# The recurrence's value projection of heads 2 and 3 moved from the stage ahead of the first mixer's slots into eight of the slots

## The chip, the core and the metric

The kernel runs on one core of a Trainium2 chip. A core has engines with an instruction stream of their own: TensorE (PE, matrix products into the accumulators called PSUM), VectorE (DVE), ScalarE (ACT), GpSimd (POOL) and the queue engine SyncE (SP), which issues transfers from the chip's memory into the core's on-chip memory. They run in parallel and wait for each other by semaphores. The metric is the device time of one execution in microseconds (us); lower is better.

## What is computed

The program is a small transformer of several layers in fp32 over 512 tokens (256 of context, 256 of latents). The change is in the first mixer, of which this is what matters: a windowed attention and a gated recurrence of four heads, both fed by slices of one projection, and joined by one output product.

```python
def even_mixer(h_ctx, h_lat, w_in, w_out, qk_g, sink, out_g, lb, cos, sin, need_ctx):
    ...
    p = split_parts(h_lat @ w_in, EVEN_PARTS)      # a_q a_k a_v b_q b_ff b_fb b_i b_g
    ...
    a_lat = window_attention(q_lat, k_lat, kv_heads(p['a_v']), k_ctx, v_ctx, sink)
    ...
    k_fw, lf_fw = gates(p['b_ff'])
    k_bw, lf_bw = gates(p['b_fb'])
    q_l = jax.nn.silu(to_heads(p['b_q'], HGRN_HEADS).astype(F32))
    i_l = to_heads(p['b_i'], HGRN_HEADS).astype(F32)
    o_fw, _ = gla_chunked(q_l, k_fw, i_l, lf_fw, s_fw)
    o_bw, _ = gla_chunked(flip(q_l), flip(k_bw), flip(i_l), flip(lf_bw), s_bw)
    b_lat = gated_head_norm(o_fw + flip(o_bw), p['b_g'], out_g)
    y_lat = jnp.concatenate([a_lat.astype(dt), b_lat.astype(dt)], axis=-1) @ w_out
```

`b_i` is the value of the recurrence: 512 columns, 128 for each of the four heads, for all 512 tokens. Head h's values are needed first where its chunk states are updated.

## The kernel before

Every engine's program is written out by hand; nothing is reordered, so each engine runs its instructions as they stand. A planner, `make_plan`, only counts: it gives each product (a "job") a PSUM bank in turn from a pool, notes which engine empties the bank (`A` for ScalarE, `V` for VectorE), and from which job on a weight tile may be overwritten. The next job in a bank waits until the job before it in that bank was emptied (`bank`). Weights come into a ring of two tiles (`RING`), loaded by SP in the order of use; `load` waits until the tile's last reader is done.

Ahead of the mixer's slots stands a stage of whole projections on TensorE: the attention's queries (`even_q`, 4 token tiles x 8 matmuls of 512 columns), its keys and values (8 products of 128 columns), the recurrence's values (`even_bi`, 4 x 8 x 512 columns), its output gates (`even_bg`, the same), and the transposes of queries and keys (`even_qkT`). `by_token` makes them, one job for each token tile. Beside it, VectorE multiplies and adds 1 MB pieces of modulation weights ("slabs", L2862): two slabs lie on chip, SP issues slab i when slab i-2 was used (`load_slabs`), on the same queue as the ring's weights. Halfway VectorE norms and rotates queries and keys (L3030 to L3066), then it goes on with slabs, and only behind the last but one of them comes its part of the slots. At two places of the stage TensorE sums a modulation group over partitions (L1332) and turns it (L1319), for which it needs VectorE's slabs and ScalarE's copies.

Then come 48 slots. The even slots 0 to 30 start an attention pair each (scores L1547, softmax on VectorE and ScalarE from L3213 and L2414, transposes L1559, output L1572); scores of the next pair wait until ScalarE has read the last pair's. Slots 0 to 31 carry in between the projections of the four recurrence heads (`fill_at`, L1589): three matmuls of 512 columns a slot, three jobs for each head (forget gates forward and backward, queries), with a ring tile of 3 x 128 columns for each head. The heads' recurrence runs a round behind the projections (`heads_at`): keys by token and scores (L1475, L1488), updates of the chunk states (L1498, the first reader of the head's values `hv`), outputs (L1508, L1515). The states are chained on VectorE (L3147, L3149). Slots 33, 34, 35, 36, 37, 40, 43 and 46 (`PARTS`) hold eight parts of the first half of the output product (`out_block`, L1538, 4 matmuls of 512 columns each), which VectorE adds to the residual (`residual_part`, L3194). In the slots the pool of banks is two: jobs take bank 0 and bank 1 in turn, whatever they are.

Of the kernel before, what the change touches and what calls it, by code (L numbers as in the profile page):

```python
# [14 lines left out]
P = 128  # L15
D = 1024
KD = D // P
# [86 lines left out]
class Plan:  # L104
# [18 lines left out]
    def add(self, stage, engine):  # L123

        b = self.pool[self.turn % len(self.pool)]
        self.turn += 1
        self.own[stage].append(self.jobs)
        self.who += engine
        self.bank.append(b)
        self.before.append(self.last.get(b))  # L130
        self.last[b] = self.jobs
        self.jobs += 1
# [123 lines left out]

def fill_at(slot):

    return [] if slot >= UNITS else [divmod(3 * (slot % PER_ROUND) + n, KD) for n in range(3)]
# [73 lines left out]
def make_plan():  # L333
# [24 lines left out]
    for slot in range(SLOTS):  # L358
# [3 lines left out]
        for j, k in fill_at(slot):  # L362
            if (j, k) == (0, 0):
                a.start(f"head{slot // PER_ROUND}")
            if k == 0:
                a.add(f"head{slot // PER_ROUND}", "A")
            if (j, k) == (2, KD - 1):
                a.tile_used()
        if slot == CAT_SLOT:
            a.start("even_out_a")  # L370
# [87 lines left out]
def first_then_second_block(nc, a, out):  # L458
# [3 lines left out]
    with ExitStack() as ctx:  # L462
# [81 lines left out]
        ePT = [view(A0 + 5120, 512), ring[:, pl.tile["even_out"] // 2 % RING, 3072:3584]]  # L544
# [256 lines left out]
        def _(sp):  # L801
# [22 lines left out]
            def load(*parts, halves=2):  # L824
# [8 lines left out]
                for p in reversed(parts):  # L833
# [4 lines left out]
                    sp.dma_start(dst, p).then_inc(signal, 96 // len(parts))  # L838
# [39 lines left out]
            for lo in (2304, 2816):  # L878
                load(wcols(ew, lo, lo + 512))
            for h in range(HG):  # L880
                load(*(wcols(ew, lo + P * h, lo + P * h + P) for lo in (1280, 1792, 768)))
# [121 lines left out]
        def _(pe):  # L1003
# [445 lines left out]
            for _ in range(2):  # L1449
                by_token(BOTH, 512, where="even")  # L1450
# [41 lines left out]
            def updates(h, d):  # L1492
                w = 2 * h + d
                pe.wait_ge(hg_kts, w + 1)
                pe.wait_ge(hg_ss, 3 * h + d + 1)
                for c in range(8):
# [78 lines left out]

            for slot in range(SLOTS):
# [6 lines left out]
                for j, kk in fill_at(slot):  # L1583
                    if (j, kk) == (0, 0):
                        stage(f"head{slot // PER_ROUND}")
                        hw = weights(3 * P)
# [3 lines left out]
                    if kk == KD - 1:  # L1590
                        ins.then_inc(acc_full, 1)
                if slot < UNITS:
# [535 lines left out]
        def _(act):  # L2128
# [203 lines left out]
            for i in BOTH:  # L2332
                evac(hv[:, i, :], 512)
# [68 lines left out]

            for slot in range(SLOTS):
                raw_inputs(slot)
                if slot == 3:
# [412 lines left out]
        def _(dve):  # L2818
# [371 lines left out]
            def residual_part(f):  # L3190

                y = filled("even_out_a", f + 1)
                for c in (1, 0):
# [798 lines left out]
```

## Time and profile before

| | us |
|---|---|
| time before, median of 3 runs | 2555.9 (2553.59 to 2556.48) |
| span of the profiled execution | 2552.4 |
| stage ahead of the slots, first product of `even_q` to the first of slot 0, on TensorE | 40.4 to 143.3 |
| slots, on TensorE | 143.3 to 352.6 |
| TensorE busy | 2481.8 (97% of the span) |
| VectorE busy | 1672.4 (66%) |
| ScalarE busy | 657.5 (26%) |

The profile lists no time of the profiled execution other than its span; the median lies 3.5 us above the span, for what is ahead of the first and behind the last recorded instruction. Only the first 390 us bear on the change. The share of 97% is an average: in the slots TensorE has idle stretches of 0.2 to 1.9 us, each with the engine that ended it. A timeline row gives the start, the length, the engine and line, the operation with its tiles and shapes, the number of instructions, and in brackets the idle time before it and what ended that. An fp32 matmul shows as two records. A row of windows gives, for a stretch, its length, the busy time of the engine asked for, the clock granted to TensorE as a share of the full one, the busy share of the transfer engines and the GB/s they moved.

### The profile page before, as it was taken

The numbers are of one execution on the slowest core, as the hardware profiler recorded it, in microseconds if no ns is written. First come the engines' busy times: TensorE is split into PE (matmuls) and PEld (weight loads), VectorE is DVE, ScalarE is ACT, GpSimd is POOL, SyncE is SP. The second block draws the span as 40 slices with busy tenths as digits, with TensorE's granted clock in tenths as the row PEclk, the third lists the DMA queues.
The fourth block names the chain that finished last, engine by engine and source line by source line (L and its number), as shares of the span: only waits on it lengthen the run. The fifth ranks groups of instructions, "written<-read, shape, count | busy, mean of one in ns | idle before, by whom it ended". The sixth has DMA issues, their size and how long they took to land.

```text
span 2552.4 us, 41132 instructions
## 1 busy us (share of the span) xinstructions
PE 2481.8 (97%) x16726; PEld 2005.8 (79%) x16726; DVE 1672.4 (66%) x3298; ACT 657.5 (26%) x1760; POOL 73.0 (3%) x96
## 2 busy tenths in 40 slices
PE   6999899999999999999999999999999999999999
PEld 3545458888888886599996867869997877868999
DVE  4967767655777645466673787657773777647785
ACT  3145512111101111122212153333321135333320
POOL 0000000000000001000000001100000000110000
PEclk9999999999999999999999999999999999999999
DMA  8532115555575868245544424135654344125563
GB/s 341 187 118 48 44 34 182 154 177 167 188 272 184 289 209 322 71 130 152 169 163 149 165 73 127 68 119 143 172 170 145 132 124 108 68 87 146 166 178 120
DMA packets 342651, 386.78 MB, mean 152 GB/s; under 512 B 8110, under 2 KB 285190, under 8 KB 330176
## 3 DMA queue, kind: packets, MB, share of 16 engines
q1 hardware_dynamic: 330896, 320.89, 40.1%
q0 software_dynamic: 8832, 57.26, 6.4%
q10 hardware_dynamic: 2736, 6.01, 0.6%
q8 instruction: 133, 2.18, 0.4%
q14 instruction: 54, 0.44, 0.1%
HBM read 383.08 MB, written 1.05 MB: 150 GB/s over the span
## 4 chain that ended last, share of the span: by engine, by line
PE 84%; DVE 9%; issue 3%; ACT 3%; DMA 2%; ACTq 0%; DVEq 0%; SPq 0%
PE acc L1032 33%; PE mx L1032 14%; PE acc L1083 10%; PE acc L1071 9%; PE acc L1093 5%; PE acc L1589 2%; PE acc L1538 1%; PE mx L1947 1%; DVE arena L3905 1%; PE mx L1398 1%; DVE hT L2894 1%; PE mx L1934 1%; PE mx L2006 1%; PE mx L1422 1%; DMA ring<-in_mod_w 0%
## 5 line engine op out<-in xcount | busy, mean ns | idle before, releaser
L1032 PE MATMUL acc<-arena 128*128 128x128 f32 (+1 forms) x2248 | 353.8, 300 | 1.0 <-ACT gate L2507 0.5
L1032 PEld LDWEIGHTS acc<-arena 128*128 128x128 f32 x2248 | 310.0, 192 | 16.8 <-ACT gate L2507 0.9
L2862 DVE SCALAR_TENSOR_TENSOR arena<-mod_w,vcols,arena 128x2048 f32<-128x2048 f32 x98 | 228.4, 2348 | 61.2 <-DMA mod_w<-in_w_ada 46.0
L1083 PE MATMUL acc<-hT,ring 128*128 128x256 f32 (+1 forms) x1024 | 249.8, 406 | 0.8 <-DVE arena L3579 0.8
L1083 PEld LDWEIGHTS acc<-hT,ring 128*128 128x128 f32 x1024 | 194.1, 190 | 54.1 <-issue 29.4
L1032 PE MATMUL acc<-hT,ring 128*128 128x128 f32 (+1 forms) x1368 | 206.1, 301 | 2.8 <-ACT hT L2255 1.4
L3255 DVE TENSOR_TENSOR arena<-ring 128x512 f32<-128x512 f32 (+1 forms) x136 | 91.7, 674 | 178.3 <-PE acc L1032 173.8
L1032 PEld LDWEIGHTS acc<-hT,ring 128*128 128x128 f32 x1368 | 184.8, 191 | 16.1 <-issue 6.4
L1071 PE MATMUL acc<-ring,hT 128*128 128x512 f32 x448 | 194.1, 593 | 2.2 <-ACT hT L2164 1.3
L1032 PE MATMUL acc<-arena,ring 128*128 128x128 f32 (+1 forms) x1256 | 194.2, 298 | 0.0
L1032 PEld LDWEIGHTS acc<-arena,ring 128*128 128x128 f32 x1256 | 171.1, 192 | 7.7 <-issue 0.8
L1032 PE MATMUL mx<-hT,ring 128*128 128x128 f32 (+1 forms) x1152 | 174.4, 296 | 1.0 <-ACT arena L2543 0.9
L1071 PEld LDWEIGHTS acc<-ring,hT 128*128 128x128 f32 x448 | 84.5, 190 | 108.7 <-issue 103.9
L1032 PEld LDWEIGHTS mx<-hT,ring 128*128 128x128 f32 x1152 | 154.9, 192 | 7.6 <-ACT arena L2543 1.2
L1032 PE MATMUL mx<-arena,ring 128*128 128x128 f32 (+1 forms) x960 | 152.7, 301 | 0.0
L1032 PE MATMUL acc<-hT,arena 128*128 128x128 f32 (+1 forms) x888 | 141.0, 302 | 0.0
L1032 PEld LDWEIGHTS mx<-arena,ring 128*128 128x128 f32 x960 | 132.8, 192 | 8.2 <-issue 2.5
L1032 PEld LDWEIGHTS acc<-hT,arena 128*128 128x128 f32 x888 | 123.6, 192 | 6.0
L1093 PE MATMUL acc<-ring,hT 128*128 128x256 f32 x384 | 96.4, 388 | 2.0 <-ACT hT L2288 0.7
L3259 DVE TENSOR_TENSOR arena<-ring 128x512 f32<-128x512 f32 (+1 forms) x136 | 92.0, 677 | 4.7
L3261 DVE TENSOR_TENSOR arena<-ring,arena 128x512 f32<-128x512 f32 (+1 forms) x136 | 92.0, 676 | 4.6
L2164 ACT ACTIVATE arena<-acc 128x512 f32<-128x512 f32 (+2 forms) x88 | 41.3, 490 | 206.6 <-PE acc L1071 122.1
(543 smaller groups left out, 3857.4 us busy)
## 6 DMA issues: line engine op xcount, KB each, us to landing
ring<-in_w_in SPq DMA_DIRECT2D x28, 2048.0 KB
mod_w<-in_w_ada POOLq DMA_DIRECT2D x48, 1024.0 KB, 5.5
ring<-in_ffn_w_in SPq DMA_DIRECT2D x88, 512.0 KB
ring<-in_w_up SPq DMA_DIRECT2D x88, 512.0 KB
mod_w<-in_mod_w SPq DMA_DIRECT2D x36, 1024.0 KB, 5.0
ring<-in_odd_w_in SPq DMA_DIRECT2D x20, 1024.0 KB
ring<-in_ffn_w_out SPq DMA_DIRECT2D x16, 1024.0 KB
ring<-in_w_down SPq DMA_DIRECT2D x16, 1024.0 KB
```

The lines of the kernel that those rows point to most:

```text
L1032: ins = nc.tensor.matmul(out, w[:, k, :], h[:, k, :], start=start and k == 0, stop=stop and k == n - 1, skip_group_check=more)
L1071: ins = nc.tensor.matmul(b[:, 0:width], src[:, k, P * i:P * (i + 1)], w[:, k, :], start=k == 0, stop=k == KD - 1)
L1083: ins = nc.tensor.matmul(b[:, 0:hi - lo], w[:, k, P * f:P * (f + 1)], hT[:, k, lo:hi], start=k == 0, stop=k == KD - 1)
L1093: ins = nc.tensor.matmul(out, a_[:, k, :], b[:, k, :], start=first and k == 0, stop=last and k == 3, skip_group_check=True)
L1398: ins = nc.tensor.matmul(mx[:, v, 0:P * (i + 1)], sqT[half, j, P * i:P * (i + 1)], skT[half, 0:P * (i + 1)], start=True, stop=True)
L1422: ins = nc.tensor.matmul(mx[half, 3, 0:P], s_v[:, b, half], pPT[o % 2][:, at:at + P], start=b == 0, stop=b == n - 1)
L1589: ins = nc.tensor.matmul(hb, hw[:, kk, P * j:P * (j + 1)], hT[:, kk, :], start=kk == 0, stop=kk == KD - 1)
L2164: ins = nc.scalar.activation(dst, src, func, **kw)
L2862: ins = V.scalar_tensor_tensor(acc_, mod_w[:, i % 2, :], vcols[:, at:at + 1], acc_, ALU.mult, ALU.add)
L3255: V.tensor_tensor(s3, a11, a10, ALU.subtract)
L3259: link(V.tensor_tensor(s2, a11, a10, ALU.subtract))
L3261: V.tensor_tensor(s4, a01, s2, ALU.subtract).then_inc(st_ws, 1)
```

## The change

The stage ahead projects the values of heads 0 and 1 only (256 of 512 columns, and half of the weights are loaded there). The value columns of heads 2 and 3 travel in those heads' ring tiles, which grow from three to four column groups of 128. In eight slots a new function, `late_values`, makes one job of 8 matmuls of 128 columns for one token tile of one head: slots 17, 20, 25 and 28 for head 2, and 32, 34, 36 and 38 for head 3. ScalarE empties each. Head 2's jobs take the bank that is next but leave the turn where it was (`between`), and count as if VectorE had emptied them; head 3's jobs, in the slots of the output parts, advance the turn. The first update of heads 2 and 3 waits for the last value. The two ring tiles are free for the output product's weights only after the last value of their head. A buffer of the attention's transposed probabilities moves from the unused end of a ring tile to memory of its own.

```diff
+LATE_VALUES = {17: (2, 0), 20: (2, 1), 25: (2, 2), 28: (2, 3), 32: (3, 0), 34: (3, 1), 36: (3, 2), 38: (3, 3)}
+EARLY_VALUES = 2 * P
...
-    def add(self, stage, engine):
+    def add(self, stage, engine, between=False):
...
-        self.turn += 1
+        if not between:
+            self.turn += 1
...
+        if slot in LATE_VALUES:
+            h, i = LATE_VALUES[slot]
+            if i == 0:
+                a.own[f"late_v{h}"] = []
+            a.add(f"late_v{h}", "V" if slot < UNITS else "A", between=slot < UNITS)
+            if i == NT - 1:
+                for half in range(2):
+                    a.released[a.tile[f"head{h}"] + half] = ("job", a.jobs)
...
-        ePT = [view(A0 + 5120, 512), ring[:, pl.tile["even_out"] // 2 % RING, 3072:3584]]
+        ePT = [view(A0 + 5120, 512), sb("probs_t1", [P, 512])[:, :]]
...
-            for lo in (2304, 2816):
-                load(wcols(ew, lo, lo + 512))
+            for lo, n in ((2304, EARLY_VALUES), (2816, 512)):
+                load(wcols(ew, lo, lo + n))
             for h in range(HG):
-                load(*(wcols(ew, lo + P * h, lo + P * h + P) for lo in (1280, 1792, 768)))
+                load(*(wcols(ew, lo + P * h, lo + P * h + P) for lo in (1280, 1792, 768, 2304)[:3 if h < 2 else 4]))
...
-            for _ in range(2):
-                by_token(BOTH, 512, where="even")
+            for width in (EARLY_VALUES, 512):
+                by_token(BOTH, width, where="even")
...
+                if h >= 2 and d == 0:
+                    late = pl.own[f"late_v{h}"][-1]
+                    emptied(late + 1, pl.who[late])
...
+            def late_values(h, i, w):
+
+                b = bank()
+                for kk in range(KD):
+                    ins = nc.tensor.matmul(b[:, 0:P], hT[:, kk, P * i:P * (i + 1)], w[:, kk, 3 * P:4 * P],
+                                           start=kk == 0, stop=kk == KD - 1)
+                ins.then_inc(acc_full, 1)
...
+                if slot in LATE_VALUES:
+                    h, i = LATE_VALUES[slot]
+                    late_values(h, i, head_w[h])
                 if slot < UNITS:
                     recurrence(slot, False)
...
-                evac(hv[:, i, :], 512)
+                evac(hv[:, i, 0:EARLY_VALUES], EARLY_VALUES)
...
+            def late_values(h, i):
+
+                if h == 2:
+                    job_ = pl.own["late_v2"][i]
+                    act.wait_ge(acc_full, job_ + 1)
+                    nc.scalar.activation(hv[:, i, P * h:P * (h + 1)], acc[:, pl.bank[job_], 0:P], ACT.Copy).then_inc(acc_v, 1)
+                else:
+                    evac(hv[:, i, P * h:P * (h + 1)], P)
...
                 raw_inputs(slot)
+                if slot in LATE_VALUES and slot < UNITS:
+                    late_values(*LATE_VALUES[slot])
+                if slot - 1 in LATE_VALUES and slot > UNITS:
+                    late_values(*LATE_VALUES[slot - 1])
...
                 y = filled("even_out_a", f + 1)
+                if f == 0:
+                    dve.wait_ge(acc_v, pl.emptied("V", pl.own["late_v2"][-1] + 1))
```

The first place is TensorE's stage ahead, the recurrence's values: `acc<-ring,hT` is a product into a bank, `x7` seven more of the kind, and in brackets stand the semaphores that an instruction waits for. Before (L1071 in `by_token`, L1332 a modulation sum):

```order
L1071 MATMUL acc<-ring,hT 128x512 [waits acc_emptied_by_scalar,weights1_in]
L1071 MATMUL acc<-ring,hT 128x512 x7
L1071 MATMUL acc<-ring,hT 128x512 [waits acc_emptied_by_scalar]
L1071 MATMUL acc<-ring,hT 128x512 x7
L1332 MATMUL mx<-arena,cond 32x512 [waits mod_rows_sb,mod_slabs_used]
L1332 MATMUL mx<-arena,cond 32x512 x7
L1071 MATMUL acc<-ring,hT 128x512 [waits acc_emptied_by_scalar]
L1071 MATMUL acc<-ring,hT 128x512 x7
```

After (the lines are L1084 and L1345 there):

```order
L1084 MATMUL acc<-ring,hT 128x256 [waits acc_emptied_by_scalar,weights1_in]
L1084 MATMUL acc<-ring,hT 128x256 x7
L1084 MATMUL acc<-ring,hT 128x256 [waits acc_emptied_by_scalar]
L1084 MATMUL acc<-ring,hT 128x256 x7
L1345 MATMUL mx<-arena,cond 32x512 [waits mod_rows_sb,mod_slabs_used]
L1345 MATMUL mx<-arena,cond 32x512 x7
L1084 MATMUL acc<-ring,hT 128x256 [waits acc_emptied_by_scalar]
L1084 MATMUL acc<-ring,hT 128x256 x7
```

The instructions and waits are the same; each value product has 256 columns in place of 512.

The second place is TensorE in slots 34 to 37: the output parts (L1538 before, L1554 after) among the updates of head 2 (L1498 and L1514), from behind the scores of slot 34 on. Before:

```order
L1538 MATMUL acc<-arena,ring 128x512 [waits acc_emptied_by_scalar]
L1538 MATMUL acc<-arena,ring 128x512 x3
L1538 MATMUL acc<-arena,ring 128x512 [waits acc_emptied_by_vector]
L1538 MATMUL acc<-arena,ring 128x512 x3
L1498 MATMUL acc<-arena 128x128 [waits hg_scores_sb,hg_kd_sb]
L1498 MATMUL acc<-arena 128x128 x7
L1538 MATMUL acc<-arena,ring 128x512 [waits acc_emptied_by_vector]
L1538 MATMUL acc<-arena,ring 128x512 x3
L1538 MATMUL acc<-arena,ring 128x512 [waits acc_emptied_by_vector]
L1538 MATMUL acc<-arena,ring 128x512 x3
```

After (L1596 is `late_values`):

```order
L1596 MATMUL acc<-ring,hT 128x128 [waits acc_emptied_by_scalar]
L1596 MATMUL acc<-ring,hT 128x128 x7
L1554 MATMUL acc<-arena,ring 128x512 [waits acc_emptied_by_vector]
L1554 MATMUL acc<-arena,ring 128x512 x3
L1554 MATMUL acc<-arena,ring 128x512 [waits acc_emptied_by_scalar]
L1554 MATMUL acc<-arena,ring 128x512 x3
L1514 MATMUL acc<-arena 128x128 [waits hg_scores_sb,hg_kd_sb]
L1514 MATMUL acc<-arena 128x128 x7
L1596 MATMUL acc<-ring,hT 128x128 [waits acc_emptied_by_vector]
L1596 MATMUL acc<-ring,hT 128x128 x7
L1554 MATMUL acc<-arena,ring 128x512 [waits acc_emptied_by_vector]
L1554 MATMUL acc<-arena,ring 128x512 x3
```

Two value jobs stand among the parts, and the turn of the banks goes with them: the part of slot 34 waits for VectorE (the residual sum of slot 33's part) where it waited for ScalarE, the value job of slot 36 waits for the residual sum of slot 34's part, and the part of slot 36 for that of slot 35's, where before it waited for that of slot 34's.

The third place is SP, from the attention's query weights on: ring weights (L838 before), key and value weights (L877), slabs (L820). Before:

```order
L838 DMA ring<-in_even_w_in 128x8x512 [waits weights_partly_used]
L877 DMA arena<-in_even_w_in 128x8x256
L820 DMA mod_w<-in_mod_w 128x2048 x2
L838 DMA ring<-in_even_w_in 128x8x512 [waits weights_partly_used]
L820 DMA mod_w<-in_mod_w 128x2048 [waits mod_slabs_used] x4
L838 DMA ring<-in_even_w_in 128x8x512 [waits acc_full]
```

After (L851, L890, L833):

```order
L851 DMA ring<-in_even_w_in 128x8x512 [waits weights_partly_used]
L890 DMA arena<-in_even_w_in 128x8x256
L833 DMA mod_w<-in_mod_w 128x2048 x2
L851 DMA ring<-in_even_w_in 128x8x256 [waits weights_partly_used]
L833 DMA mod_w<-in_mod_w 128x2048 [waits mod_slabs_used] x4
L851 DMA ring<-in_even_w_in 128x8x512 [waits acc_full]
```

Nothing changes place; the load between the second and the third slab is 1 MB in place of 2 MB.

## Rows read from the trace of the kernel before

**Rows 1.** Chain of waits, stage ahead: start us, us, engine, tile, line, instructions.

```profile
40.52 55.58 PE acc L1071 x224
...
105.45 34.35 PE acc L1071 x80
```

**Rows 2.** Timeline of ScalarE in the stage ahead, key and value products and after.

```profile
69.89 0.28 ACT L2164 ACTIVATE arena<-acc 128x128 f32<-128x128 f32 x1 [1.19 <-PE acc L1071]
...
82.40 0.28 ACT L2164 ACTIVATE arena<-acc 128x128 f32<-128x128 f32 x1 [1.51 <-PE acc L1071]
...
97.99 0.33 ACT L2218 ACTIVATE st<-st,eps 128x40 f32<-128x40 f32 x1 [14.02 <-DVE st L3031]
```

**Rows 3.** Timeline of VectorE, stage ahead and the first pair's softmax.

```profile
59.41 14.05 DVE L2862 SCALAR_TENSOR_TENSOR arena<-mod_w,vcols,arena 128x2048 f32<-128x2048 f32 x6 [3.68 <-issue]
...
81.90 9.33 DVE L2862 SCALAR_TENSOR_TENSOR arena<-mod_w,vcols,arena 128x2048 f32<-128x2048 f32 x4 [3.29 <-DMA mod_w<-in_mod_w]
...
146.85 0.69 DVE L3214 TENSOR_REDUCE st<-mx 128x2 f32<-128x512 f32 x1 [0.96 <-PE mx L1547]
```

**Rows 4.** Windows: us, VectorE busy, TensorE's granted clock, transfer share, GB/s.

```profile
48.00:52.00 4.00, 3.89 (x3) 1.00 1.04 408
```

**Rows 5.** Timeline of TensorE, slot 0's projection and slot 2's scores.

```profile
143.29 2.81 PE L1589 MATMUL acc<-hT,ring 128*128 128x512 f32 x6 [0.84 <-ACT arena L2164]
...
149.44 0.70 PE L1547 MATMUL mx<-arena 64*128 64x256 f32 x4
```

**Rows 6.** Timeline of TensorE, idle stretches of slots 18 to 30.

```profile
218.34 0.63 PE L1475 MATMUL acc<-fconst,arena 128*128 128x128 f32 x4 [0.47 <-DVE mod_w L3149]
...
234.22 0.63 PE L1559 MATMUL mx<-fconst,arena 128*128 128x128 f32 x4 [1.87 <-ACT arena L2432]
...
263.96 0.63 PE L1475 MATMUL acc<-fconst,arena 128*128 128x128 f32 x4 [0.52 <-DVE mod_w L3149]
...
274.34 1.16 PE L1498 MATMUL acc<-arena 64*128 64x128 f32 x16 [1.66 <-ACT arena L2372]
...
281.56 0.63 PE L1559 MATMUL mx<-fconst,arena 128*128 128x128 f32 x4 [1.87 <-ACT arena L2432]
```

**Rows 7.** Windows of slots 29 and 30, TensorE: us, busy, granted clock.

```profile
282.00:284.00 2.00, 2.00 (x7) 0.60 0.03 8
284.00:286.00 2.00, 2.00 (x3) 0.55 0.00 0
```

**Rows 8.** Timeline of TensorE, pair scores of slots 26 and 30, slot 30's projection.

```profile
257.93 1.13 PE L1547 MATMUL mx<-arena 64*128 64x512 f32 x4
...
282.12 1.85 PE L1547 MATMUL mx<-arena 64*128 64x512 f32 x4
283.90 3.78 PE L1589 MATMUL acc<-hT,ring 128*128 128x512 f32 x6
```

**Rows 9.** Timeline of VectorE, slots 32 to 39.

```profile
301.12 0.69 DVE L3230 COPY ring<-mx 128x512 f32<-128x512 f32 x1 [4.22 <-PE mx L1559]
...
313.54 0.87 DVE L3194 SCALAR_TENSOR_TENSOR x<-acc,mb,x 128x256 f32<-128x256 f32 x2
...
323.86 0.87 DVE L3194 SCALAR_TENSOR_TENSOR x<-acc,mb,x 128x256 f32<-128x256 f32 x2
...
332.80 0.74 DVE L3131 COPY_PREDICATED arena<-bconst,acc 128x512 f32<-128x512 uint8 x1
```

**Rows 10.** Timeline of TensorE, slots 34 to 44.

```profile
311.17 8.08 PE L1538 MATMUL acc<-arena,ring 128*128 128x512 f32 x16
...
320.84 3.70 PE L1538 MATMUL acc<-arena,ring 128*128 128x512 f32 x8 [0.50 <-DVE x L3194]
324.79 3.70 PE L1538 MATMUL acc<-arena,ring 128*128 128x512 f32 x8 [0.24 <-DVE x L3194]
...
331.00 1.75 PE L1515 MATMUL acc<-mod_w,arena 128*64 128x128 f32 x28
...
344.86 1.13 PE L1508 MATMUL acc<-arena,mod_rows 128*128 128x128 f32 x8 [1.03 <-DVE mod_w L3149]
```

More of the change, by code:

```diff
@@ L837, in load @@
                     signal = w_in[t // 2 % RING] if halves == 2 else h_in[t % (2 * RING)]
-                    sp.dma_start(dst, p).then_inc(signal, 96 // len(parts))
+                    sp.dma_start(dst, p).then_inc(signal, 96 // len(parts) if len(parts) < 4 else 48 if p is parts[0] else 16)
             def load_unit(w, c):
@@ L1574, in pair_out @@
                 ins.then_inc(att_o, 1)
+            def late_values(h, i, w):
[4 more added lines that the diff above has]
+                ins.then_inc(acc_full, 1)
+            head_w = {}
             for slot in range(SLOTS):
@@ L1585, in _ @@
                         stage(f"head{slot // PER_ROUND}")
-                        hw = weights(3 * P)
+                        hw = head_w[slot // PER_ROUND] = weights(3 * P if slot < 2 * PER_ROUND else 4 * P)
                     if kk == 0:
```

## Prediction

> **What bounds the kernel now.** I read the chain of waits first, then the timelines of the four engines around the places that the change touches, then TensorE's granted clock in 2 us windows. In the stage ahead the chain is TensorE alone, 55.58 us up to the first modulation sum and 34.35 us from the third value product to the end of the gates [rows 1]. A reader would conclude that work taken from there comes off the time. The other timelines say no. ScalarE stands 14.02 us waiting for VectorE [rows 2]. VectorE itself waits for the value of nothing that TensorE's projections make: its idle stretches are 3.68 us and 3.29 us for slabs that have not landed, and only at 146.85 does it wait for TensorE, 0.96 us, for the first scores [rows 3]. Two engines run neck and neck, and the chain shows the one that is ahead by a hair. In the slots TensorE is the bound with gaps: 0.47, 1.87, 0.52, 1.66 and 1.87 us, each ended by VectorE or ScalarE [rows 6]. From slot 32 on it is the other way about again: VectorE waits 4.22 us for the last transposes, then works through with hardly a gap, and TensorE waits for it [rows 9, 10].
>
> **What goes from the stage ahead.** 80 records, that is 40 matmuls of 512 columns, take 34.35 us [rows 1]: 0.859 us each. Thirty-two value matmuls lose half of their columns: 32 x 0.429 = 13.7 us off TensorE. What of it reaches the end is set by VectorE. The scores of slot 2 at 149.44 [rows 5] need ScalarE's probabilities of pair 0, and these need VectorE at 146.85, behind seven slabs. VectorE gains two things. The 0.96 us of waiting goes, since the first scores come early. And the first slab wait gets shorter: the value weights are issued ahead of that slab on the same queue, the transfers move 408 GB/s there [rows 4], and 1.05 MB less in front of it are 2.6 us, which fits into the 3.68 us of waiting [rows 3]. If the later slabs keep pace, all VectorE work up to slot 0 moves by 2.6 us, and with the wait by 3.5 us. If the slab of the 3.29 us wait, which lies behind the gates' 2 MB, lands when it did, the first gain is eaten there and 1.0 us is left. I take 3.5, since that queue is served in order and holds 1 MB less.
>
> The other 10.2 us of TensorE's 13.7 become waiting, half of it ahead of the turn at L1319 (its copies come from ScalarE, behind VectorE's norms) and half, about 5 us, ahead of the scores of slot 2. After 1.66 and 1.87 us of idle time within 10 us the granted clock goes to 0.60 and 0.55, that is towards the lower of its two levels, 1.2 GHz [rows 6, 7]. The scores then took 1.85 us instead of 1.13 [rows 8] and a projection 3.78 [rows 8] instead of 2.81 [rows 5]: 0.72 + 0.97 = 1.7 us. I take one such fall behind the 5 us wait, in slots 2 and 3, which TensorE bounds. **Front: -3.5 + 1.7 = -1.8 us, ends -3.5 and +0.7** (1.0 of gain with the fall).
>
> **What the slots get.** A product of 8 matmuls of 128 columns: ScalarE empties the eight key and value products between 69.89 and 82.40, seven steps of 1.79 us [rows 2]. Eight of them are 14.3 us, so TensorE's work grows by 0.6 us in all; ScalarE's emptying is 0.28 us each [rows 2], and it waits elsewhere. A small product costs no more for a column than a wide one here: 4 x 1.79 = 7.15 us against 8 x 0.859 = 6.87.
>
> The Trainium skill, "TensorE: Matmul & The Clock Gate", section "Back-to-back issue gap", speaks against such a split: it gives about 81 ns for a matmul of 128 columns and 131 ns for one of 512 in a stream, so four small ones would take 2.5 times a wide one, and by that estimate the eight jobs would cost 34 us in place of 14.3. The measured rows are of this shape and type, and they decide.
>
> *Slots 17 and 20.* The value job stands behind the slot's projection, where neither VectorE nor ScalarE waits for TensorE. 3.58 us more work, and the gaps of 0.47 and 1.87 us behind it [rows 6] close: **+1.2 us** (ends +0.5 and +1.8). What the next slots' engines need comes later by this and they follow, as TensorE is their bound up to slot 25.
>
> *Slots 25 and 28.* 3.58 us again, against gaps of 0.52, 1.66 and 1.87 us [rows 6], together 4.05: **0**, with 0.5 us of the last gap left. The low clock of slot 30 came behind the two long gaps, and they are gone: **-1.7 us** (ends -1.7 and 0), since TensorE is busy from there to slot 31.
>
> *Slot 32.* The job stands ahead of the last attention output and transposes, for which VectorE waits 4.22 us at 301.12 [rows 9]. No cover: **+1.8 us**.
>
> *Slots 34 to 38.* Three jobs of 1.79 us, but the price is the turn of the two banks. Before, the part of slot 34 waits for a copy of ScalarE that is long done, the part of slot 36 for the residual sum of slot 34's part, and starts at 320.84. Now it waits for the residual sum of slot 35's part, which VectorE makes at 323.86 and ends at 324.73 [rows 9]; VectorE's own list is unchanged there, and the value job of slot 36 fits ahead of it. The stretch from 320.84 to the end of head 2's outputs, 331.00 + 1.75, is 11.91 us, with 0.24 us of waiting at 324.79 that goes [rows 10] and the last value job that comes: 324.73 + 11.91 - 0.24 + 1.79 = 338.2 against 332.75. VectorE's masked scores begin at 332.80, when these outputs are done [rows 9], and from there it is the chain to the outputs of head 3, which wait for it 1.03 us [rows 10]. **+5.4 us.** The low end: if VectorE's sum of slot 35's part were no hindrance, TensorE's row counts: 3 x 1.79 = 5.37, less the gaps of 0.50 and 0.24, less 1.2 us that the two parts at 311.17 lost to a low clock (8.08 for 8 matmuls [rows 10], 6.87 by rows 1): 3.4. The high end has one more clock fall, 7.1.
>
> *At nothing.* The weights of the output product's second half may load only behind slot 38, still ahead of the slots' end. The buffer moved out of the ring costs no instruction. The waits added to updates and to the first residual sum are for jobs several slots back.
>
> **Sum.** -1.8 + 1.2 + 0 - 1.7 + 1.8 + 5.4 = +4.9 us on the span of 2552.4: 2557.3; the median of the runs lies 3.5 us higher, so 2560.8, or +0.19%. Behind the slots nothing changes.
>
> **The rivals.**
> *The work only fills gaps.* The stage ahead gives its whole 13.7 us, as its chain [rows 1] says: -13.7 + 1.2 - 1.7 + 1.8 + 5.4 = -7.0, or 2548.9. Against it stand VectorE's rows: with a start only 3.5 us earlier it cannot hand over pair 0 sooner. Chance 0.06. The Trainium skill, "Perfetto Trace Analysis", section "Optimization Strategy", says that interleaving stages with different bounds may pay, which is this case; the trace agrees only in part, as both engines are full in the stage ahead.
> *The banks cost nothing.* The front keeps 3.5 us without a clock fall and the tail costs its low end: -3.5 + 1.2 - 1.7 + 1.8 + 3.4 = +1.2, or 2557.1. For it: the fall in slot 2 is inferred from one place only [rows 6 to 8]. Against it: the sum at 323.86 stands behind VectorE's own work, not behind TensorE [rows 9]. Chance 0.26.
> *Slower: the tail runs at the low clock.* TensorE, once it waits in slots 34 and 36 for VectorE, is granted the lower clock for the parts behind, which are now the chain, and slot 30 keeps its fall: +4.9 + 1.7 + 1.7 = +8.3, or 2564.2. It decides as soon as the two waits reach what stood ahead of 282 [rows 6]. Chance 0.24.
> *The change does not do what it says.* The last weights come too late for the second half of the output product. The load is issued only behind slot 38, some 40 us later than before (about 340 against a place right behind 301 [rows 9]); no row shows one that late, so 0.04, slower by some 5 us more.
> The forecast has 0.40.
>
> **The numbers.** A difference of 0.2%, 5.1 us, is about what can be told from no change. Half of the forecast's case lies below 5.1 and half above, the second rival lies within, the third and fourth above: faster 0.08, same 0.46, slower 0.46. The range leaves out the first rival and the end of the third: 2554.5 to 2566.
>
> **What would show it.** Right: VectorE's first slab wait near 1 us; slot 0's first projection near 134 with about 5 us of waiting ahead of the scores of slot 2 and these near 146; the gap ahead of 234 closed; a full clock in slot 30; VectorE's masked scores of head 3 some 5 us later against its copy of slot 32. Wrong: if slot 2's scores start at 140 or before, VectorE was not the gate; if the part of slot 36 starts without waiting for a residual sum, the bank turn is not the price; if no clock fall shows in slots 2 and 3, the front is worth 3.5.

## The result and the profile after

The changed kernel takes 2562.8 us (median of 5 runs, 2560.1 to 2567.7) against 2555.8 (5 runs, 2552.6 to 2556.5): a ratio of 1.0039, 95% interval 1.0028 to 1.0050. The forecast was 2560.8. Its profiled execution has a span of 2560.9 us, 8.5 more than before; TensorE is busy 2485.5 us, 3.7 more, VectorE 1672.7, 0.3 more. So more than half of the 8.5 us is waiting of TensorE. In every run the listed time lies 1.8 us above the span of the same execution, and not 3.5: the profiled execution of before was then some 1.7 us quicker than the median, so shifts between the traces come out larger than those of the medians, 8.5 us against 7.0.

Where it arises, by starts on TensorE (and VectorE's masked scores of head 3) in the two traces:

| start, us | before | after | shift | step since the row above |
|---|---|---|---|---|
| slot 0, projection | 143.29 | 137.10 | -6.19 | |
| slot 2, scores | 149.44 | 147.07 | -2.37 | +3.82 |
| slot 17, projection | 209.91 | 209.26 | -0.65 | +1.72 |
| slot 22, projection | 235.84 | 237.69 | +1.85 | +2.50 |
| slot 31, projection | 290.70 | 291.62 | +0.92 | -0.93 |
| slot 32, last transposes | 300.00 | 302.90 | +2.90 | +1.98 |
| masked scores of head 3 | 332.80 | 341.08 | +8.28 | +5.38 |
| first transposes behind the slots (L1295, L1308) | 352.57 | 360.84 | +8.27 | -0.01 |

Timeline of TensorE after (start, length, engine and line, operation, instructions; in brackets the idle time ahead and what ended it), the turn of the modulation and slots 0 to 3, which answer [rows 5]:

```profile
100.34 1.04 PE L1332 MATMUL mx<-fconst,mod_rows 128*128 128x128 f32 x4 [4.36 <-ACT mod_rows L2209]
...
137.10 2.81 PE L1614 MATMUL acc<-hT,ring 128*128 128x512 f32 x6 [0.84 <-ACT arena L2192]
...
147.07 0.70 PE L1563 MATMUL mx<-arena 64*128 64x256 f32 x4 [3.75 <-ACT st L2458]
147.70 4.54 PE L1614 MATMUL acc<-hT,ring 128*128 128x512 f32 x6
```

Of the 13.7 us that TensorE gave back, slot 0 starts 6.2 us earlier. The rest went ahead of it: the 4.36 us wait, one of 1.45 us at 90.40, and about 1.7 us by a low clock at 100 (windows below). Behind it 3.75 us more of waiting follow in slot 2. The timeline of VectorE after says for whom it waits ([rows 3]):

```profile
57.50 14.05 DVE L2903 SCALAR_TENSOR_TENSOR arena<-mod_w,vcols,arena 128x2048 f32<-128x2048 f32 x6 [1.33 <-issue]
...
81.02 9.33 DVE L2903 SCALAR_TENSOR_TENSOR arena<-mod_w,vcols,arena 128x2048 f32<-128x2048 f32 x4 [4.46 <-DMA mod_w<-in_mod_w]
...
144.92 0.69 DVE L3257 TENSOR_REDUCE st<-mx 128x2 f32<-128x512 f32 x1
```

The first slab wait fell from 3.68 to 1.33, the second grew from 3.29 to 4.46, and the slab behind it begins at 81.02 instead of 81.90. The 0.96 us of waiting ahead of the first reduction are gone, as forecast. The first slab's start is 1.91 us earlier (59.41 to 57.50), and 0.88 of it outlive the second wait.

The windows after (length, TensorE busy, granted clock as a share of full, transfer share, GB/s), which answer [rows 7]:

```profile
100.00:102.00 2.00, 1.66 (x6) 0.62 0.00 0
102.00:104.00 2.00, 2.00 (x6) 0.53 0.00 0
148.00:150.00 2.00, 2.00 (x4) 0.56 0.87 211
150.00:152.00 2.00, 2.00 (x4) 0.58 0.00 0
282.00:284.00 2.00, 1.94 (x4) 1.00 0.35 68
```

The clock falls right behind each of the two long waits, to 0.53 to 0.62 as a mean of these windows, towards the lower level of 1.2 GHz. The fall behind 3.75 us stretched a projection from 2.84 us to 4.54; the one behind 4.36 us lies ahead of more waiting, so what it cost TensorE did not reach the end. The fall of slots 29 and 30, and one that the trace of before has at 308 to 314, are gone.

The slots with head 2's jobs, TensorE and then ScalarE after ([rows 6]):

```profile
211.84 1.95 PE L1596 MATMUL acc<-ring,hT 128*128 128x128 f32 x16
...
217.34 1.12 PE L1614 MATMUL acc<-hT,ring 128*128 128x512 f32 x2 [0.37 <-ACT arena L2436]
...
228.01 1.95 PE L1596 MATMUL acc<-ring,hT 128*128 128x128 f32 x16
...
233.89 1.98 PE L1614 MATMUL acc<-hT,ring 128*128 128x512 f32 x4 [0.37 <-ACT arena L2436]
236.07 0.63 PE L1575 MATMUL mx<-fconst,arena 128*128 128x128 f32 x4 [0.19 <-ACT arena L2473]
```

```profile
217.01 0.28 ACT L2436 ACTIVATE arena<-acc 128x128 f32<-128x128 f32 x1 [2.25 <-PE acc L1614]
...
233.56 0.28 ACT L2436 ACTIVATE arena<-acc 128x128 f32<-128x128 f32 x1 [6.74 <-PE acc L1614]
```

The late job at 228.01 is over at about 230, and ScalarE's copy of it comes at 233.56, released by L1614, a projection, and not by L1596, the late job itself. Then a projection waits for that copy. This wait is new, and the prediction did not have it. (The releaser is inferred from semaphores; e2_count below tests it.)

The tail, VectorE and then TensorE after ([rows 9, 10]):

```profile
304.03 0.69 DVE L3273 COPY probs_t<-mx 128x512 f32<-128x512 f32 x1 [6.20 <-PE mx L1575]
...
316.43 0.87 DVE L3237 SCALAR_TENSOR_TENSOR x<-acc,mb,x 128x256 f32<-128x256 f32 x2
...
326.92 0.87 DVE L3237 SCALAR_TENSOR_TENSOR x<-acc,mb,x 128x256 f32<-128x256 f32 x2
...
341.08 0.74 DVE L3172 COPY_PREDICATED arena<-bconst,acc 128x512 f32<-128x512 uint8 x1 [4.61 <-PE acc L1531]
```

```profile
317.36 7.13 PE L1554 MATMUL acc<-arena,ring 128*128 128x512 f32 x16 [1.88 <-DVE x L3237]
325.51 2.05 PE L1596 MATMUL acc<-ring,hT 128*128 128x128 f32 x16
327.84 7.13 PE L1554 MATMUL acc<-arena,ring 128*128 128x512 f32 x16 [0.28 <-DVE x L3237]
...
339.27 1.75 PE L1531 MATMUL acc<-mod_w,arena 128*64 128x128 f32 x28
```

The parts wait for residual sums that end at 317.30 and 327.79, and VectorE, which before had the outputs of head 2 on time, waits 4.61 us for them.

### The profile page after: what moved, and what is told of

It is laid out like the page before. It is cut to its first block, busy times and chain, and to the rows that moved or that the text cites. A ratio compares the mean times of both kernels' runs of the same rounds, so it can differ in the third digit from the quotient of the medians.

```text
span 2560.9 us, 41399 instructions
## 1 busy us (share of the span) xinstructions
PE 2485.5 (97%) x16854; PEld 2020.8 (79%) x16854; DVE 1672.7 (65%) x3298; ACT 659.1 (26%) x1768; POOL 73.2 (3%) x96
## 4 chain that ended last, share of the span: by engine, by line
PE 81%; DVE 10%; DMA 3%; issue 3%; ACT 2%; SPq 0%; ACTq 0%; DVEq 0%
PE acc L1045 33%; PE mx L1045 14%; PE acc L1096 10%; PE acc L1106 5%; PE acc L1084 5%; PE acc L1614 3%; DMA mod_w<-in_mod_w 2%; PE acc L1554 2%; DVE arena L2903 1%; PE mx L1975 1%; DVE arena L3948 1%; PE mx L1411 1%; DVE hT L2935 1%; PE mx L1962 1%; PE mx L2034 1%
## 5 line engine op out<-in xcount | busy, mean ns | idle before, releaser
L1084 PE MATMUL acc<-ring,hT 128*128 128x512 f32 (+1 forms) x448 | 181.8, 566 | 3.0 <-ACT hT L2192 1.3
L1084 PEld LDWEIGHTS acc<-ring,hT 128*128 128x128 f32 x448 | 85.5, 192 | 97.2 <-issue 90.6
L1614 PE MATMUL acc<-hT,ring 128*128 128x512 f32 x192 | 92.6, 616 | 3.0 <-ACT arena L2192 1.5
```

Source lines behind the costliest of these rows:

```text
L1084: ins = nc.tensor.matmul(b[:, 0:width], src[:, k, P * i:P * (i + 1)], w[:, k, :], start=k == 0, stop=k == KD - 1)
L1614: ins = nc.tensor.matmul(hb, hw[:, kk, P * j:P * (j + 1)], hT[:, kk, :], start=kk == 0, stop=kk == KD - 1)
```

## The experiments

Ratios are against the kernel before, run alongside it on the same chip; a median is of 4 (e2) to 11 executions, a ratio's interval about 0.1% to either side. The shifts are of the profiled executions against the trace of before. A stage's start varies by some 0.5 to 1 us between executions of one kernel (the first product of `even_q`, ahead of which nothing is changed, starts between 39.4 and 41.1), so differences within a row tell more than its level. The rest of the program adds scatter of its own: from the masked scores to the end of the span the profiled executions gain up to 1.9 us on before or lose up to 6.1.

| run | median us | ratio (95%) | slot 2 scores | slot 17 | slot 22 | slot 31 | last transposes | masked scores |
|---|---|---|---|---|---|---|---|---|
| after | 2562.8 | 1.0039 (1.0028, 1.0050) | -2.37 | -0.65 | +1.85 | +0.92 | +2.90 | +8.28 |
| e1_front | 2554.2 | 0.9998 (0.9989, 1.0008) | -2.46 | +0.59 | +0.61 | +0.64 | +0.63 | +1.24 |
| e2_count | 2565.4 | 1.0045 (1.0030, 1.0060) | -0.69 | +2.47 | +3.32 | +1.71 | +3.68 | +10.22 |
| e3_banks | 2561.4 | 1.0027 (1.0016, 1.0038) | -2.48 | -0.80 | +1.70 | +0.78 | +2.75 | +5.45 |
| e4_spare | 2561.4 | 1.0028 (1.0017, 1.0038) | -1.30 | -1.27 | +1.23 | +0.32 | +2.29 | +8.83 |
| e5_head2 | 2553.0 | 0.9996 (0.9987, 1.0005) | -1.06 | -0.94 | -0.09 | -1.73 | -1.74 | -1.12 |
| e6_head3 | 2560.9 | 1.0027 (1.0016, 1.0038) | -1.62 | +1.30 | +1.31 | +1.31 | +3.29 | +8.67 |
| e7_head2_spare | 2552.6 | 0.9996 (0.9987, 1.0004) | +0.14 | +1.81 | +2.66 | +1.02 | +1.01 | +1.01 |
| e8_all | 2557.2 | 1.0010 (1.0001, 1.0019) | -2.69 | -2.56 | -1.72 | -3.36 | -1.39 | +2.94 |
| e9_front_load | 2554.3 | 1.0000 (0.9990, 1.0009) | -2.38 | -0.68 | -0.69 | -2.33 | -2.34 | -2.34 |
| e10_front_slab | 2547.2 | 0.9974 (0.9964, 0.9984) | -6.12 | -6.11 | -6.11 | -7.77 | -7.78 | -7.79 |
| e11_head2_slab | 2549.2 | 0.9977 (0.9968, 0.9986) | -5.32 | -4.70 | -3.85 | -5.50 | -5.50 | -5.50 |
| e12_all_slab | 2555.6 | 1.0005 (0.9996, 1.0014) | -6.78 | -6.16 | -5.32 | -6.96 | -4.99 | -0.73 |

**The front alone.** The eight late jobs are left out.

```diff
-LATE_VALUES = {17: (2, 0), 20: (2, 1), 25: (2, 2), 28: (2, 3), 32: (3, 0), 34: (3, 1), 36: (3, 2), 38: (3, 3)}
+LATE_VALUES = {}
...
-                                           hv[half, c // 2, P * h:P * (h + 1)], start=True, stop=True)
+                                           hv[half, c // 2, P * (h % 2):P * (h % 2 + 1)], start=True, stop=True)
```

> The stage ahead projects the values of heads 0 and 1 only, with half of the weights, and the late value jobs are left out (heads 2 and 3 read the values of heads 0 and 1), so only the first half of the change is left. Theory (VectorE's slabs are the gate, its start moves 1.9 us, TensorE's low clock gives back 1.7): slot 2's scores at 147.1, the low clock behind them, the projection of slot 16 0.6 to 0.7 us earlier than before, and a time of about 2555 (2553.5 if the low clock at 282 stays away). Rival (TensorE's 13.7 us in the stage ahead are the bound): slot 2's scores near 136, time near 2542.

Thirteen microseconds of TensorE's work are gone, and the time is that of before (the interval allows 2.8 us less to 2.0 more). The scores of slot 2 come 2.46 us earlier, a low clock behind them, from 146 to 154, takes that back, and nothing is left at slot 17.

**The count that ScalarE waits for.** A late job of head 2 is numbered behind the projection that runs through the slot's end, but is finished ahead of it. Its copy waits until as many products are finished as its own number says, so for that projection too. Here the copy waits for one product fewer, and the copy of the running projection for one more.

```diff
                 if r < HG and s in (3, 6):
+                    if r in (2, 3):
+                        act.wait_ge(acc_full, pl.own[f"head{r}"][s // 6] + 2)
                     evac(hf[s // 6][r % 2], 512)
...
-                    act.wait_ge(acc_full, job_ + 1)
+                    act.wait_ge(acc_full, job_)
```

> As the changed kernel, but ScalarE's copy of head 2's late values waits for the count that the value job itself reaches, and no longer for the head's running product behind it. Theory (in the slots 17 to 28 the surplus over the forecast comes from this wait, which holds up the next product in the bank and ScalarE's list): the four bank waits of 0.37 us go, the transposes behind slot 20 start about 1.2 us earlier, those behind slot 28 about 2 us, time 2560.8. Rival (the jobs themselves cost it): no change, 2562.8.

ScalarE's copy now follows the late job, and the projection and transposes behind no longer wait (ScalarE, then TensorE, of this kernel; its marks lie some 3 us later than those of after at slot 17):

```profile
232.49 0.28 ACT L2438 ACTIVATE arena<-acc 128x128 f32<-128x128 f32 x1 [2.53 <-PE acc L1596]
```

```profile
234.99 2.74 PE L1614 MATMUL acc<-hT,ring 128*128 128x512 f32 x6
237.57 0.60 PE L1575 MATMUL mx<-fconst,arena 128*128 128x128 f32 x4
```

From slot 17 to slot 22 the shift grows by 0.85 us instead of 2.50, from there to slot 31 it falls by 1.61 instead of 0.93: 2.3 us in all. Every other kernel with this edit (e5, e7, e8, e11, e12) shows +0.84 or +0.85 and -1.64 or -1.65 as well. The mechanism stands. The time did not fall, though: this execution kept the low clock of slots 2 and 3 longer (148 to 156), had another one at 318 to 324, and its span was 6 us longer again behind the slots, which the change doesn't touch. More than 4 of these 6 us arise at one place, a wait for weights of a later layer, with a granted clock of 0.50 to 0.65 from 926 to 930 behind it:

```profile
926.21 3.44 PE L1045 MATMUL acc<-ring,hT 128*128 128x256 f32 x8 [3.53 <-DMA ring<-in_odd_w_in]
```

In the trace of before that wait is 0.80 us; e3 lost some 4 us there by a wait of 3.01. Why the transfer came late in these two executions isn't known. By its time alone (four executions) e2 can't be told from the changed kernel.

**Other banks for head 3.** Three of its jobs get two banks of the other group and stand outside the turn.

```diff
+OWN_BANK = ((3, 1), (3, 2), (3, 3))
...
-                b = bank()
+                own = (h, i) in OWN_BANK
...
+                b = mx[:, 2 + i % 2, :] if own else bank()
```

> As the changed kernel, but the value jobs of slots 34, 36 and 38 write PSUM banks that nothing else uses there, so that the output parts take their two banks in the old turn. Theory (turn of the banks: waits for VectorE's residual sums): the part of slot 34 starts 1.9 us earlier, right behind its value job, and the outputs of head 2 end 2.0 us earlier: 2560.8. Rival (three jobs of 1.8 us on a full TensorE): no change, 2562.8.

From the last transposes to the masked scores the loss is 2.70 us in place of 5.38. The medians, 2561.4 and 2562.8, are too near each other to show it. The parts no longer wait for a residual sum (TensorE of this kernel; compare 317.36 and 327.84 above):

```profile
313.29 2.05 PE L1609 MATMUL mx<-ring,hT 128*128 128x128 f32 x16
315.18 7.03 PE L1564 MATMUL acc<-arena,ring 128*128 128x512 f32 x16
...
323.23 2.05 PE L1609 MATMUL mx<-ring,hT 128*128 128x128 f32 x16
325.12 7.03 PE L1564 MATMUL acc<-arena,ring 128*128 128x512 f32 x16
```

So half of the tail's price is the turn of the banks, and half is the jobs themselves, in two executions whose clock stayed full there. It is not a fixed share: e8 and e12, with the same banks, had the clock low somewhere from 304 to 314 and lost 4.33 and 4.26 us, while the old turn cost e6 5.38 with a low clock at 314 to 318.

**Work in the wait of slot 2.** Eight idle matmuls of 256 columns ahead of its scores, to see what the low clock behind costs.

```diff
             for slot in range(SLOTS):
+                if slot == 2:
+                    spare(mx[:, 3, 0:256], 8)
```

> As the changed kernel, with 8 idle matmuls of 256 columns (3.6 us) ahead of the scores of slot 2, in TensorE's 3.75 us of waiting there. Theory (the low clock at 148 comes from that waiting): granted clock 1.00 in 148 to 152, the projection of slot 2 takes 2.8 us instead of 4.5, and all behind is 1.7 us earlier: 2561.1. Rival (VectorE or ScalarE would hold slots 3 and 4 anyway): clock full, but no gain, 2562.8.

```profile
144.59 3.62 PE L1362 MATMUL mx<-fconst 128*128 128x256 f32 x16
148.14 0.70 PE L1563 MATMUL mx<-arena 64*128 64x256 f32 x4
148.77 2.84 PE L1616 MATMUL acc<-hT,ring 128*128 128x512 f32 x6
```

With the wait filled, the projection behind takes 2.84 us and not 4.54: the fall costs 1.7 us, the price that was taken. The spare work ran past the end of the wait (the scores come 1.07 us later than in after), so only 0.6 us of it shows at slot 17. A fall at 318 to 322 took that back later:

```profile
318.00:320.00 2.00, 2.00 (x4) 0.54 0.00 0
```

The two parts there took 8.83 us in place of 7.13, and from the last transposes to the masked scores this execution lost 6.54 us in place of 5.38; e2 lost 6.54 by the same fall.

**One head at a time.** Head 2 alone, with the count of e2; and head 3 alone. The early product then has 384 columns.

```diff
+LATE_VALUES = {17: (2, 0), 20: (2, 1), 25: (2, 2), 28: (2, 3)}
+VALUE_AT = (0, 1, 3, 2)
+EARLY_VALUES = 3 * P
```

> Only head 2's values are late (slots 17, 20, 25, 28), with the corrected count; heads 0, 1 and 3 are projected in the stage ahead (384 columns). Theory (the loss is in the slots 32 to 38, which hold head 3's jobs): slots 34 to 44 as in the kernel before, the stretch from slot 17 to slot 31 0.8 us shorter than before, the front within 1 us of before: 2554, no difference to before that can be told. Rival (any late job costs its 1.8 us): 7 us of jobs against 6.9 us saved, of which 2.4 arrive: about 2559.

```diff
+LATE_VALUES = {32: (3, 0), 34: (3, 1), 36: (3, 2), 38: (3, 3)}
+EARLY_VALUES = 3 * P
```

> Only head 3's values are late (slots 32, 34, 36, 38), heads 0, 1 and 2 are projected in the stage ahead. Theory: slots 17 to 31 as in the kernel before, slot 32 +2.0, slots 34 to 38 +5.4 against before, time 2561 to 2562. Rival (the loss lies in the slots 17 to 31): about 2555.

Head 2's move costs nothing that can be told (0.9996). Head 3's costs 0.27%, and its steps are those of the whole change to the hundredth: +1.98 in slot 32, +5.38 from there to the masked scores.

**Spare work with head 2 alone, and everything mended.** e7 is e5 with five of the idle matmuls; e8 is the whole change with the count, the banks and five idle matmuls.

```diff
+                if slot == 2:
+                    spare(mx[:, 3, 0:256], 5)
```

> As the kernel with head 2 alone late, with 5 idle matmuls of 256 columns (2.3 us) ahead of the scores of slot 2. Theory (the low clock behind that wait takes back what the front gains): full clock at 146 to 152, 1 to 2 us less than without them, about 2552.5, that is 1 to 2 us less than before. Rival (VectorE holds the slots behind anyway): as without them.

> The changed kernel with the corrected count, head 3's jobs of slots 34 to 38 in banks of their own, and 5 idle matmuls ahead of the scores of slot 2. Theory: the parts add up: -2.3 in slots 17 to 31, -2.0 to -2.7 in slots 34 to 38, -1 to -2 in the front: 2557, still 2 us above before, since slot 32's 2.0 us and 3 us of slots 34 to 38 remain. Rival (they share one slack): 2560.

In e7 the idle matmuls ended 2.64 us ahead of the scores, the clock still fell at 150 to 154, and nothing was won. In e8 1.60 us were left and it did not fall there; the whole change is down to 2557.2, from 2562.8, and still not faster than before. None of e2, e3 and e4 differs from the changed kernel by its time beyond the intervals; the three edits together do (1.0010 against 1.0039).

**What holds the front: the load?** e1 again, but with the full 2 MB of value weights loaded as before; only the products are narrower.

```diff
-            for lo, n in ((2304, EARLY_VALUES), (2816, 512)):
+            for lo, n in ((2304, 512), (2816, 512)):
```

> As the kernel with only the first half of the change (256 value columns in the stage ahead, the late jobs left out, heads 2 and 3 read the values of heads 0 and 1), but the whole 2 MB of value weights is loaded there. Theory (the shorter load moves VectorE by 0.9 us, the rest of its 1.9 us is the wait for the first scores that goes): slot 2's scores at 148 instead of 147, VectorE's first slab wait back at 3 us or more. Rival (the load has no part in it): 147, as with the short load.

```profile
58.85 9.34 DVE L2900 SCALAR_TENSOR_TENSOR arena<-mod_w,vcols,arena 128x2048 f32<-128x2048 f32 x4 [3.64 <-issue]
...
81.05 9.34 DVE L2900 SCALAR_TENSOR_TENSOR arena<-mod_w,vcols,arena 128x2048 f32<-128x2048 f32 x4 [3.28 <-DMA mod_w<-in_mod_w]
```

The first slab wait is back at 3.64, the slab behind the second begins at 81.05 (81.02 in after), slot 2's scores come 2.38 us earlier than before (2.46 in e1), and the ratios are 1.0000 and 0.9998. The rival held: the shorter load moves the first slab and can't be seen behind the second. A part of a microsecond stays open, since this execution's first product of `even_q` came earlier than the others' (39.57, 40.02 in after, 40.62 in e1).

This run has no late job, and its two gaps of 1.66 and 1.87 us ahead of slot 30 are those of before. The clock stayed full there all the same:

```profile
280.88 0.63 PE L1572 MATMUL mx<-fconst,arena 128*128 128x128 f32 x4 [1.87 <-ACT arena L2470]
```

```profile
282.00:284.00 2.00, 2.00 (x8) 1.00 0.03 8
```

So did it in e10, with the same gaps; in both the shift falls by 1.65 us from slot 22 to slot 31 without any job moved.

**What holds the front: VectorE.** e1 again, with slabs 14 and 15 worked on for 64 of their 2048 columns, the rest left out.

```diff
+                            w_ = 64 if i in (14, 15) else 2048
```

> As the kernel with only the first half of the change and without late jobs, and VectorE's last two slabs before and behind pair 0 are worked on 64 of 2048 columns only (left out, 9 us of VectorE). Theory (VectorE's slabs are what holds the front): slot 2's scores come right behind slot 1's projection, at 143 to 144, no waiting and no low clock there, slot 16's projection 5 to 6 us earlier than before: 2549 to 2550. Rival (ScalarE or the transfers hold the front): scores stay at 147, time 2554.

VectorE and TensorE of this kernel:

```profile
139.14 0.48 DVE L2901 SCALAR_TENSOR_TENSOR arena<-mod_w,vcols,arena 128x64 f32<-128x64 f32 x2 [0.30 <-DMA mod_w<-in_mod_w]
...
140.74 0.69 DVE L3253 TENSOR_REDUCE st<-mx 128x2 f32<-128x512 f32 x1 [1.04 <-PE mx L1560]
```

```profile
143.32 0.70 PE L1560 MATMUL mx<-arena 64*128 64x256 f32 x4
143.96 2.84 PE L1611 MATMUL acc<-hT,ring 128*128 128x512 f32 x6
```

The wait ahead of the scores is gone, the clock stays full there, and the scores come 6.1 us earlier instead of 2.4. All of it lasts, slot 30's fall stays away besides, and the time falls by 7.1 us. VectorE's slabs were the gate.

**The two together, nothing left out.** Slab 14 moves to slot 1 and slab 15 to slot 3; what uses their sums follows two slots later. e11 does it on e5, e12 on e8 without the idle matmuls.

```diff
-            mod_slabs(2 * KD - MOD_EARLY - 1)
+            mod_slabs(2 * KD - MOD_EARLY - 2)
...
-                if slot == 1:
+                if slot in (1, 3):
                     mod_slabs(1)
-                if slot == 3:
+                if slot == 5:
                     recurrence_buffers()
```

> As the kernel with head 2 alone late and the corrected count, and VectorE's last slab ahead of the slots moved behind pair 0 (the two last slabs in slots 1 and 3, the modulation sum and turn two slots later), nothing left out. Theory (VectorE's slabs hold the front, and in the slots it has room for one): slot 2's scores right behind slot 1's projection, 3 us or more earlier than before (147 to 146), slots 17 to 31 0.8 us shorter, tail as before: 2550.5, faster than both. Rival (the slab only shifts the wait into slots 2 to 6): about 2553, as without the move.

> As the changed kernel (heads 2 and 3 late) with the corrected count, head 3's jobs in banks of their own and the same move of the slab, without idle matmuls. Theory: front -6, slots 17 to 31 -0.8, slot 32 +2.0, slots 34 to 38 +2.7 to +4.3: -0.5 to -2 against before, 2552 to 2554. Rival (the front's gain does not get through): 2557 as without the move.

TensorE of e11, and its windows at that place:

```profile
144.12 0.70 PE L1564 MATMUL mx<-arena 64*128 64x256 f32 x4
144.75 2.84 PE L1615 MATMUL acc<-hT,ring 128*128 128x512 f32 x6
148.13 0.44 PE L1576 MATMUL mx<-fconst,arena 128*128 128x128 f32 x2 [0.54 <-DVE arena L3271]
```

```profile
148.00:150.00 2.00, 1.87 (x6) 1.00 1.20 290
```

e11 takes 2549.2 us, against 2554.7 for before, run alongside it: 0.23% faster, where e5, which differs by the slabs alone, was 0.04% faster. It is faster than both kernels. With head 3's jobs as well (e12), 6.2 us of its 7.0 us of lead are spent between slot 31 and the masked scores; forecast were 0.5 to 2 us less than before, measured is 0.9 more, no difference that can be told. The move of the slab without the change was not run. In the trace of before slot 2's scores follow right behind the projection, without a wait for VectorE [rows 5], so little is to be expected of it alone, but that is not shown.

## Why the prediction was near, and which of its steps were not

The direction held, and the size nearly (+4.9 us forecast; +7.0 by the medians, +8.5 by the spans), but two steps were wrong and both erred to the same side, by 1.2 and 2.0 us, and one term that came out was partly luck. The measured 2562.8 lies a little nearer to the slower rival's 2564.2 than to the forecast's 2560.8. A slip stands in its chances: by its own cases faster and slower add up to 0.06 and 0.48, not 0.08 and 0.46.

*The front, -1.8 forecast, -0.65 measured.* That VectorE sets the end, that slot 2's scores wait, and the price of the low clock (1.7) were right. The step that failed is "I take 3.5, since that queue is served in order and holds 1 MB less". Its own low end described what happened: the gain at the first slab is eaten at the next. The rows of the DMA queue tell more (issues, after and then before):

```profile
67.83 0.41 SPq L851 DMA_DIRECT2D ring<-in_even_w_in  x1
71.58 5.34 SPq L833 DMA_DIRECT2D mod_w<-in_mod_w  x2
```

```profile
69.19 0.41 SPq L838 DMA_DIRECT2D ring<-in_even_w_in  x1
...
73.49 5.47 SPq L820 DMA_DIRECT2D mod_w<-in_mod_w  x2
```

The queue had run empty before these loads, at 60, and was full again behind the gates' 2 MB (windows after):

```profile
60.00:62.00 2.00, 2.00 (x6) 1.00 0.00 0
76.00:78.00 2.00, 2.00 (x21) 1.00 1.08 432
```

So a megabyte less ahead of the first slab saves no transfer time for the second. What counts there is when the gates' weights are issued, and these wait for TensorE: they go into the ring tile that the queries' products read, and the next products on TensorE begin 0.24 us ahead of that issue:

```profile
67.59 14.45 PE L1084 MATMUL acc<-arena,hT 128*128 128x128 f32 x128
```

The same 0.24 us stand in e1, e2, e3, e4, e8, e10 and e12; in before the issue stood right behind that of a slab (69.19). So of 1.9 us won at the first slab only 1.36 could pass. From that issue to the second slab's use 12.71 us passed before and 13.19 after, within the 12.0 to 13.9 of the fourteen traces. The first projection of slot 0 came at 137.10, not "near 134", since 7.5 us of the freed time became the two waits ahead of it and the low clock.

*Slots 17 to 20, +1.2 forecast, +2.50 measured; slots 25 to 28, 0 against +0.7.* The step that failed is costing ScalarE's emptying at 0.28 us and nothing else. Its wait counts finished products, and the order in which jobs are numbered is not the order in which they finish. With the count mended, the terms are +0.85 (within the forecast's ends of 0.5 and 1.8) and 0.0. "The gap ahead of 234 closed" held nearly (0.19 us are left), but for the same reason new gaps of 0.37 stand inside the projections.

*The low clock of slot 30, -1.7.* The size is right: the projection at 285.75 takes 2.84 us in place of 3.78, and the windows at 282 show 1.00. With the 0.7 above it is the -0.93 of the table. The reason, that the gaps ahead are gone, is only half shown: none of the nine traces with head 2's late jobs has this fall, but of the five without them, all with both gaps, three have it (before, e1, e6) and two don't (e9, e10).

*Slot 32, +1.8.* Measured 1.98.

*The tail, +5.4.* Measured 5.38, by the mechanism named: the part of slot 36 starts at 327.84, 0.05 us behind the end of the residual sum that begins at 326.92. Its two halves are measured now, at full clock: 2.7 for the turn of the banks (e3), 2.7 for the jobs, where the low end had 3.4. That the tail of after had no fall was luck: e2 and e4 have the same tail, had one, and lost 6.54 us there.

*The price of a narrow product.* Eight late jobs took 1.95 to 2.05 us by their rows, with the start of what follows 1.78 us behind (211.84 to 213.62). The Trainium skill, "TensorE: Matmul & The Clock Gate", section "Back-to-back issue gap", by whose figures for a stream (81 and 131 ns) eight of them come to an estimated 34 us, doesn't fit this shape and type: the trace disagrees, at 14.2 us.

The sum of the steps is -0.65 + 2.50 - 0.93 + 1.98 + 5.38 = 8.28 us, the shift of the masked scores. Of the rivals, "the work only fills gaps" fell with e1: of the front's 13.7 us none shows in the time. "The banks cost nothing" fell with e3, by its trace. The slower one came near in time, 2564.2, but in the profiled execution not by its mechanism: no low clock shows in the tail of after, and slot 30's fall is gone. It does show in the tails of before and of all runs but e3, e7 and e11, somewhere between 302 and 324. In e2 and e4 such a fall cost 1.2 us, where this rival had 1.7. When it comes there, and how many of the executions behind the median had it, stays open.

## What to carry to other kernels

Ask of the engine on the chain how far behind it the next one runs: here 13.7 us off TensorE were worth nothing while VectorE was full (e1), and moving one VectorE slab made head 2's half of it worth 0.2% (e11). Where a job is slipped between two others, look at who counts finished jobs, and at who gets its buffer next: the wait of the count cost 2.3 us, the turn of the banks up to 2.7, neither being work. Move work to where its own engine waits, not merely to a stage with another bound: head 2's jobs cost nothing that can be told (e5), head 3's stood where everyone waited for TensorE (e6).

## What the runs showed that was not expected

The granted clock fell towards 1.2 GHz behind waits of 4.36 and 3.75 us (0.53 to 0.62 in the windows of after, 0.50 in e1), and where the one of slot 2 was filled (e4) or removed (e10, e11) it did not fall there. It is not the same from one execution to the next: behind the same wait of 4.36 us it was low from 100 to 104 in after and from 100 to 108 in e2, and behind the same two gaps ahead of slot 30 it fell in before and not in e9. In e11, where the wait at 101 was 1.60 us, it did not fall. A slab that was issued 1.9 us earlier, with 1 MB less ahead of it on its queue, was there 0.9 us earlier, since the loads right ahead of it waited for TensorE.
